# Hybrid Conformer and sparse-attention block on eight cores: eight K/V weight chunks loaded once, and a compression MLP that reads a regrouped copy

## The reference, cut to what matters

```python
u = rms_norm(x, norm_mix_pre)
proj = u @ w_in
(glu_in, q, kc, vc, ks, vs, kw, vw, nsa_gates, gate_a, gate_b) = jnp.split(proj, offsets, axis=-1)
...
def compress_blocks(kv, pos, w1, w2):
    chunks = kv.reshape(B, S // CMP_STRIDE, CMP_STRIDE, G, d)
    blocks = jnp.concatenate([chunks[:, i:i + n_cmp] for i in range(r)], axis=2)
    blocks = blocks + pos[None, None, :, None, :]
    blocks = blocks.transpose(0, 1, 3, 2, 4).reshape(B, n_cmp, G, CMP_BLOCK * d)
    return jax.nn.gelu(blocks @ w1) @ w2
```

## Time and profile before

| | us |
|---|---|
| median of 3 runs | 7516.69 (7505.12 to 8146.9) |
| the profiled execution | 7526.77 |
| span of its slowest core, core 0 | 7525.3 |
| spans of the eight cores | 7501.8 to 7525.3 |
| TensorE matmuls busy | 7161.9 (95%) |
| DVE busy | 2399.1 (32%) |
| ACT busy | 1033.8 (14%) |
| POOL busy | 454.3 (6%) |

### The profile page before, as it was taken

One profiled execution on the slowest core, in us unless ns is written; L12 is line 12 of the kernel. 1 busy time (PEld: TensorE's weight loads), 2 busy tenths in 40 slices (PEclk: granted clock), 3 DMA queues, 4 the chain that ended last, 5 costly groups with the idle time before them and its releaser, 6 DMA issues.

```text
span 7525.3 us, 114930 instructions; the slowest of 8 cores (7501.8 to 7525.3 us)
## 1 busy us (share of the span) xinstructions
PE 7161.9 (95%) x44684; PEld 4301.7 (57%) x44956; DVE 2399.1 (32%) x4557; ACT 1033.8 (14%) x2035; POOL 454.3 (6%) x729
## 2 busy tenths in 40 slices
PE   6889999979999999999989999999999999999996
PEld 2356544434544544446656666666666666666664
DVE  4458865414444441232551111111111111111144
ACT  2100000113333330001331100010000100011100
POOL 0000000000000000001100000000000000000010
PEclk9999999889999999999999999999999999999998
DMA  8954454567776335556974455876678766643697
GB/s 190 229 102 84 91 102 97 125 124 132 120 128 113 69 70 128 118 115 220 305 222 87 78 111 117 132 113 110 154 155 127 113 122 151 141 78 74 229 314 252
DMA packets 324967, 1042.73 MB, mean 139 GB/s; under 512 B 27568, under 2 KB 113456, under 8 KB 299088
## 3 DMA queue, kind: packets, MB, share of 16 engines
q0 software_dynamic: 162256, 716.37, 49.8%
q1 hardware_dynamic: 162176, 318.98, 13.2%
HBM read 1410.78 MB, written 206.57 MB: 215 GB/s over the span
## 4 chain that ended last, share of the span: by engine, by line
PE 83%; DMA 9%; DVE 3%; issue 2%; ACT 1%; SPq 1%; DVEq 0%; ACTq 0%; POOLq 0%
PE bank L997 49%; PE bank L298 23%; PE bank L1029 6%; DMA xs_67<-xo_t 2%; DMA out<-xf_64956 2%; PE bank L782 2%; PE bank L542 2%; PE bank L760 1%; SPq L118 1%; DMA p_kv<-sgb_70 1%; DMA part_63_64955<-p_y 1%; DVE obf_12100 L821 1%; DMA p_x<-xsE_32300 0%; DMA xs_67<-xc_t 0%; DMA qT_12091<-p_q 0%
## 5 line engine op out<-in xcount | busy, mean ns | idle before, releaser
L997 PE MATMUL bank<-merged_29150,wslot 128*128 128x336 bf16 (+1 forms) x15168 | 2199.0, 308 | 7.2 <-DMA wslot<-w_out_b 5.5
L298 PE MATMUL bank<-uT_65,wslot 128*128 128x512 bf16 (+1 forms) x9643 | 1978.3, 363 | 50.8 <-DVE uT_65 L403 26.7
L997 PEld LDWEIGHTS bank<-merged_29150,wslot 128*128 128x128 bf16 x15168 | 1484.8, 98 | 720.8 <-issue 8.6
L997 PE MATMUL bank<-actq_37395,wslot 128*128 128x352 bf16 (+1 forms) x12288 | 1783.9, 309 | 3.7 <-DVE yr_64953 L1269 3.4
L997 PEld LDWEIGHTS bank<-actq_37395,wslot 128*128 128x128 bf16 x12288 | 1203.8, 98 | 583.7 <-issue 5.5
L298 PEld LDWEIGHTS bank<-uT_65,wslot 128*128 128x128 bf16 x9792 | 967.9, 99 | 986.5 <-issue 96.3
L1173 DVE SCALAR_TENSOR_TENSOR rlE_32302<-bank,acc_57_32303 128x336 f32<-128x336 f32 (+1 forms) x384 | 197.0, 513 | 1525.9 <-PE bank L997 1525.5
L450 DVE SCALAR_TENSOR_TENSOR yb_2668<-glu_2667,cps,yb_2668 128x1024 f32<-128x1024 f32 x480 | 616.0, 1283 | 44.1 <-DVE yb_2668 L450 0.9
L1178 ACT ACTIVATE actq_37395<-rlE_32302 128x336 bf16<-128x336 f32 (+1 forms) x384 | 187.0, 487 | 2878.2 <-DVE rlE_32302 L1173 2878.2
L763 ACT ACTIVATE emt_12097<-bank 128x512 bf16<-128x512 f32 (+1 forms) x736 | 343.4, 519 | 372.4 <-PE bank L760 252.5
L1226 DVE TENSOR_TENSOR ost_38524<-bank,part_38523 128x336 f32<-128x336 f32 (+1 forms) x192 | 98.6, 513 | 790.5 <-PE bank L997 785.9
(11 more groups left out here) (174 smaller groups left out, 3184.7 us busy)
## 6 DMA issues: line engine op xcount, KB each, us to landing
wslot<-w_in_t POOLq DMA_DIRECT2D x158, 1024.0 KB, 10.3
wslot<-w_up_t POOLq DMA_DIRECT2D x122, 1024.0 KB, 11.0
wslot<-w_out_b POOLq DMA_DIRECT2D x96, 1024.0 KB, 7.6
wslot<-w_dn_t POOLq DMA_DIRECT2D x96, 1024.0 KB, 11.6
wslot<-w_dn_b POOLq DMA_DIRECT2D x96, 1024.0 KB, 8.5
p_y<-ost_38524 SPq DMA_DIRECT2D x96, 512.0 KB, 4.5
xs_67<-xo_t SPq DMA_DIRECT2D x64, 528.0 KB, 11.7
w_out_b<-w_out_t POOLq DMA_DIRECT2D x32, 1024.0 KB, 18.0
```

What stands on the lines that cost most here:

```text
L298: fns = [lambda kc=kc, bk=bk: nc.tensor.matmul(bk[:, 0:n], wt[:, kc * 128:(kc + 1) * 128], rhs[:, kc, lo:lo + n], start=(kc == 0), stop=(k ...
L997: fns = [lambda kc=kc: nc.tensor.matmul(bk[:, 0:n], wt[:, kc * 128:(kc + 1) * 128], rhs[:, kc, lo:lo + n], start=(kc == 0), stop=(kc == KC ...
```

## The change

In phase A0 chunks 16 to 23 are loaded once: the context group of a chunk runs, and one chunk later its two groups of own tokens, evacuated by ACT and stored (`evac_own`). Phase A1 leaves these eight chunks out. `own_norm` gets 3 steps per tick and 8 empty steps, and is exhausted before the first own group. The compression MLP loads one chunk ahead into a single `csrc`, ACT copies it into `csd` grouped by offset, and the matmuls read 127 consecutive elements of `csd`. `comp_gen` takes eight steps per group and two steps per tick; GLU ticks take 3, 3 and 4 steps of `conv_gen`. By counting steps, phase A1's second part has 66 ticks; `comp_gen` ends at tick 55, the apply part falls in ticks 59 to 66.

```diff
-    def dense(ch, rhs, rhsB, groups, evac, tick=None, parts=1):
-        wt, wb = load_w(w_in_t[ch])
+    def dense(ch, rhs, rhsB, groups, evac, tick=None, parts=1, w=None):
+        wt, wb = w if w is not None else load_w(w_in_t[ch])
...
-            for _ in range(4):
+            for _ in range(8):
                 yield
             rstd_of(acco, accoB, TE)
...
-            for _ in range(3 if tk[0] % 4 == 0 else 2):
+            for _ in range(3):
                 next(gen, None)
+
+        def evac_own(ci):
+            def evac(gi, bk, bb, lo, n):
+                i = sctr[0] % 4
+                sctr[0] += 1
+                K.op(act, lambda: nc.scalar.activation(out=sgb[:, i, :], in_=bk[:, 0:n], func=AF.Identity), r=[bb], w=[sgbB[i]])
+                K.dma(sp, p_kv[ci, :, 1024 + lo - 32:1024 + lo - 32 + n], sgb[:, i, :], r=[sgbB[i]], w=[kvoB[ci]])
+            return evac
...
+        late = None
         for ci in range(16, 24):
-            dense(CH_KV + ci, uc, ucB, [(512, 512)], evac_kv(ci), tick)
-        for _ in gen:
-            pass
+            w = load_w(w_in_t[CH_KV + ci])
+            dense(CH_KV + ci, uc, ucB, [(512, 512)], evac_kv(ci), tick, w=w)
+            if late is not None:
+                for _ in gen:
+                    pass
+                dense(0, uT, uTB, [(32, 512), (544, 512)], evac_own(late[0]), w=late[1])
+            late = (ci, w)
+        dense(0, uT, uTB, [(32, 512), (544, 512)], evac_own(late[0]), w=late[1])
...
-        csrc = Tile("csrc", [128, 2, 2048], BF16, w1.end)
+        csrc = Tile("csrc", [128, 2048], BF16, w1.end)
+        csd = Tile("csd", [128, 16, 128], BF16, csrc.end)
...
+        def load_c(i):
+            if i < 8:
+                K.dma(sp, csrc[:], p_kv[i], r=[kvcB[i], kvoB[i]], w=[csrcB])
...
         def comp_gen():
+            load_c(0)
...
-                    src, sB = csrc[:, g % 2, :], csrcB[g % 2]
-                    K.dma(sp, src, p_kv[a * 4 + g], r=[kvcB[a * 4 + g], kvoB[a * 4 + g]], w=[sB])
+                    K.op(act, lambda: nc.scalar.copy(out=csd[:], in_=csrc[:].rearrange("p (n s) -> p s n", s=16)), r=[csrcB], w=[csdB])
+                    load_c(a * 4 + g + 1)
                     yield
-                    v3 = src.rearrange("p (n s) -> p n s", s=16)
+                    yield
+                    yield
...
-                            rhs = v3[:, 0:127, l] if l < 16 else v3[:, 1:128, l - 16]
+                            rhs = csd[:, l, 0:127] if l < 16 else csd[:, l - 16, 1:128]
...
+        def tick3():
+            t3n[0] += 1
+            ticks(4 if t3n[0] % 3 == 0 else 3)()
...
-            dense(CH_GLU + 2 * c, uT, uTB, tg3, evac_a, ticks(3))
-            dense(CH_GLU + 2 * c + 1, uT, uTB, tg3, evac_b, ticks(3))
+            dense(CH_GLU + 2 * c, uT, uTB, tg3, evac_a, tick3)
+            dense(CH_GLU + 2 * c + 1, uT, uTB, tg3, evac_b, tick3)
...
         def tick2():
             t4()
             next(cgen, None)
+            next(cgen, None)
...
-        for ci in range(8, 24):
+        for ci in range(8, 16):
             dense(CH_KV + ci, uT, uTB, tg2, evac_store(p_kv[ci, :, 1024:2048], kvoB[ci]), tick2)
```

More of the change, by code:

```diff
@@ L508, in phase_A1 @@
         w1 = Tile("w1", [128, 8192], BF16, cstg.end)
-        csrc = Tile("csrc", [128, 2, 2048], BF16, w1.end)
-        w2 = Tile("w2", [128, 256], BF16, csrc.end)
+        csrc = Tile("csrc", [128, 2048], BF16, w1.end)
+        csd = Tile("csd", [128, 16, 128], BF16, csrc.end)
+        csdB = csd.buf()
+        w2 = Tile("w2", [128, 256], BF16, csd.end)
         posb = Tile("posb", [128, 64], BF16, w2.end)
@@ L514, in phase_A1 @@
         cb = Tile("cb", [128, 4], F32, hid.end)
-        w1B, csrcB, w2B, posB, gxB, hidB, cbB = w1.buf(), csrc.bufs(2), w2.buf(), posb.buf(), gx.buf(), hid.buf(), cb.buf()
+        w1B, csrcB, w2B, posB, gxB, hidB, cbB = w1.buf(), csrc.buf(), w2.buf(), posb.buf(), gx.buf(), hid.buf(), cb.buf()
+        def load_c(i):
+            if i < 8:
+                K.dma(sp, csrc[:], p_kv[i], r=[kvcB[i], kvoB[i]], w=[csrcB])
         def comp_gen():
+            load_c(0)
             K.dma(pool, posb[:], posT[:, :], w=[posB])
@@ L544, in comp_gen @@
                                 start=(l == 0), stop=(l == 31)))
-                        K.group(pe, fns, r=[sB, w1B], w=[bb])
+                        K.group(pe, fns, r=[csdB, w1B], w=[bb])
                         x_, t_ = gx[:, 0, 0:127], gx[:, 1, 0:127]
@@ L584, in ticks @@
             return tick
+        t3n = [0]
+        def tick3():
+            t3n[0] += 1
+            ticks(4 if t3n[0] % 3 == 0 else 3)()
         tg3 = [(0, 352), (352, 352), (704, 352)]
```

## The result

| | before | after |
|---|---|---|
| median of the runs, us | 7516.05 (4 runs) | 7428.01 (4 runs) |
| the profiled execution, us | 7526.77 | 7427.62 |
| span of its slowest core, us | 7525.3 (core 0) | 7426.1 (core 1) |
| start of the first attention matmul, median of the eight cores, us | 1651.1 | 1563.9 |
| TensorE busy, us | 7161.9 | 7068.6 |

The ratio of the runs is 0.9884 [0.9861, 0.9906]: 88 us less, 1.2%, inside the range forecast (7360 to 7455) and 19 us above its 7409. Up to the first attention matmul 87.2 us went (the table); behind it nothing is edited. Yet the time behind it (median span of the eight cores less that start) runs from 5850 to 5864 us over the seven kernels here in which nothing behind it is edited, so up to 14 us of a difference in the whole time can come from there.

The account below looks back on a forecast made before the run. TensorE bounds the kernel, its busy time hiding slow strided reads in 512 compression matmuls. 144.4 us off and 36 on, net 108, took the 7516.7 us median to 7409 us; range 7360 to 7455.

Parts of the forecast that it names:

- Phase A0: Shared weight loads make `uT` whole at about 356 us instead of 412: 7 us off, between 0 and 14.5.
- GLU stage: 20 convolution steps per channel block instead of 18; DVE just fits beside TensorE: 2 us on, bounds 0 to 36.
- The rival in which DVE bounds this stage: GLU stage: a convolution step takes 1.5 us, costing 36 us instead of 2, 7443 us; chance 0.06.
- Compression stretch: Compression MLP: contiguous matmuls 90 us off, recovered clock 30, no `csrc` wait 17.4; added waits 6 and 1 on.
- the added waits: Compression MLP: TensorE waits for `hid` behind DVE's convolution steps, 6 us on; late weights, 1 us on.
- the slot of the next query chunk: After the keys' last group, query chunk weights queue behind `w1` and `w2` on POOL: 1 us on, bounds 0 to 8.
- The end of phase A1: The apply part slides beside POOL's casts and gate weights where DMA is full, delaying `qT`: 27 us on.
- The sign named for it: At the end, TensorE waits 50 to 60 us for `qT` and the transposes ahead, where it was 28.8.
- the full addition: End of phase A1: DMA engines only add the apply part's 36.6 us of transfers, making `qT` 36 us later.
- the end takes more: End of phase A1: full addition plus store latencies between SP's instructions, delay 45 us, 7427 us; chance 0.11.
- the stride is not what makes L542 slow: First compression product: something else slows its matmuls, so 90 and 30 us are gone: 7528 us; chance 0.03.
- The copy is slow: Compression MLP: ACT's strided copy takes 8.7 us, 21 us past its cover over eight copies: 7430 us; chance 0.08.

## Why the prediction was right, and which term was off

The forecast (within 2%, faster) held; the sum was 108 us and 88 came. It had called a difference within 2% about what can't be told from none, but the interval of the ratio, 0.9861 to 0.9906, leaves 1 out clearly. On the profiled cores, up to the first attention matmul, 1656.6 - 1573.9 = 82.7 us went, and they come apart by stage:

- **Phase A0, 7 forecast, 8.3 measured.** The GLU stage starts at 412.6 us before and at 514.8 after, with 16 groups of own tokens, 110.5 us, ahead of it. `uT` was whole at 359.8 (the last write starts at 358.5), forecast 356. The working held: a longer wait at L316 and a shorter one for `uT`.
- **GLU stage, 2 forecast, 0 measured.** TensorE is busy for all of its 460 us, with DVE at 393.57 where it was 359.75. The rival in which DVE bounds this stage fell.
- **Compression stretch, 130.4 forecast (90 + 30 + 17.4 - 6 - 1), 118.9 measured.** At 110.5 / 16 = 6.907 us a dense group, 82 groups before took 178.1 us more than their due (744.5 us, from 873.4 to 1617.9) and 66 after took 78.5 more (534.4 us, from 975.5 to 1509.9), of which 19.3 belong to the end, below: 178.1 - 59.2. The matmuls gave 120.5 - 31.4 = 89.1 us against 90, the clock came back, 0.98 against 0.89, and `csrc` no longer waits; with the added waits below, the 118.9 us leave some 30 us for the clock, as forecast. The short groups don't lower it, as was assumed. What was too small are the added waits: `hid` 11.7 instead of 6, since one at the end of a convolution block took 5.87 us (the other seven add up to 5.8, the forecast's 0.8 apiece). The bounds named that place, but not what happens there: DVE stood 5.92 us waiting for ACT's square of the finished block (L476) at 1353.18, which was queued on ACT behind the evacuation (1352.68) of the dense group still running. Also the slot of the next query chunk 4.3 instead of 1; and behind these two the dense matmuls took 1.9 and 1.3 us more than at full clock (15.89 against 13.97 for 64, 8.35 against 7.07 for 32), which the sum had left out.
- **The end of phase A1, 27 forecast, 64.0 - 38.7 + 19.3 = 44.6 measured.** From the end of the compression stretch to the first attention matmul it was 38.7 us before (1617.9 to 1656.6) and is 64.0 after (1509.9 to 1573.9), with 19.3 more inside the stretch: the 16.3 us stop and the slow group behind it.

The term that was furthest off is the last of the sum, "the end of phase A1". Its form held: `qT` stands on SP behind the last `p_conv` store; against the last dense group it was issued 56.3 - 7.6 = 48.7 us later and landed 23.3 us quicker, since POOL's casts were done by then, 25.3 us net. The sign named for it, a wait of 50 to 60 us for `qT` and the transposes ahead of it, came as 43.6 + 4.9 + 4.6 = 53.1 us. Two things in it were off. Its size: the forecast stayed under the full addition of the apply part's 36.6 us, and the 45 of the rival "the end takes more" is what came. The casts and the loads of POOL were part of the reason given, and moving six casts showed it: 69.4 us of stops became 33.7. But the store latencies that the rival adds are not shown to be the rest, since four store buffers won nothing; the 8 us over the full addition stay open. And the place: 19.3 of the 44.6 us lie ahead of the last dense group, where no term and no sign had them. There the SiLUs of the apply part wait for their transfers on ACT, the evacuations stand behind them, and four banks don't carry TensorE over that. I had asked which transfers collide, but not what is queued on ACT behind an instruction that waits for one. (No kernel with more banks, or with the evacuations on another engine, was run; by the chain above, TensorE would then only reach its wait for `qT` sooner.)

Of the other rivals, "the stride is not what makes L542 slow" fell to the kernel that keeps the stride alone (120.5 us again). "The copy is slow" fell as a price, not as a mechanism (its ratio, 235 / 55, would be 235 / 61 = 3.9 with the contiguous matmul as measured). The groups of ACT that copy `csd`, first in the changed kernel, then in the kernel that copies in order:

```profile
L554 ACT COPY csd_3322<-csrc_3321 128x2048 bf16<-128x2048 bf16 x8 | 31.4, 3919 | 0.0
```

```profile
L554 ACT COPY csd<-csrc 128x2048 bf16<-128x2048 bf16 x8 | 15.1, 1890 | 0.0
```

The strided copy takes 3.92 us, just over the upper bound of 3.8, and fits its cover of 6.9 us, so TensorE never waits for it. The price of the 32-byte step differs by engine: 2.1 times on ACT and, 235 ns against 1.96 us / 32 = 61, nearly four times on TensorE. The Trainium skill, SBUF — State Buffer ("Door 1: The DMA port swizzle"), says that each access that crosses to a new 16-byte line pays a penalty. That a step of 32 bytes costs agrees with it on both engines; where the line lies no run here shows, since only steps of 2 and of 32 bytes were compared.

## What to carry to other kernels

A busy engine can hide a slow read: compare the time of a matmul with others of its shape before taking 95% busy for a bound, and look at the clock behind it. Work that leaves a stage takes its ticks with it, so side work paced by those ticks slides to the end: ask what it will meet there, on the DMA engines and behind it on each engine's queue. When a wait names a buffer, give it more buffers once: if the wait moves to the next transfer, the time stays and the DMA share is near full (0.93 to 0.96 here), look to throughput before buffers.

## What was not expected

- Moving a load past a crowded stretch can make it four times as quick: `qT` landed in 30.85 us before and in 7.5 us after, the same 0.5 MB, when no packet of the casts was left beside it.
- A stop costs more than its length: 32 dense matmuls behind a 16.3 us stop took 9.94 us instead of 7.07, the first 4 us of them at a granted clock of 0.50.
- DVE at 393.57 of 460 us, in order and with work due in every tick, made TensorE wait not once there.
